# A new opening of a two-branch encoder layer: column groups for the gate rows, two key tiles in the modulation stages, and x scaled by token before it is transposed

## The reference

```python
mod = silu(c) @ w_ada + b_ada                      # six vectors of 1024: sh1, sc1, g1, sh2, sc2, g2
h = rmsnorm(x, norm_mix) * (1 + sc1) + sh1
proj = h @ w_in                                    # hq, hf, hi, hog, gq, gk, gv, ga, gb, gz, gate_a, gate_b
q, k, v = silu(causal_conv(gq, gk, gv))            # four taps; q and k are then l2-normed per head
log_a = -exp(a_log) * softplus(ga + dt_bias)       # ga, gb: 4 columns each, one per head
beta = sigmoid(gb)
y = sigmoid(gate_a) * (o_hg @ w_pa) + sigmoid(gate_b) * (o_gdn @ w_pb)
x = x + g1 * (y @ w_out)
x = x + g2 * swiglu(rmsnorm(x, norm_ffn) * (1 + sc2) + sh2)
```

## Time and profile before

| | |
|---|---|
| median of 3 runs | 943.8 us (943.55 to 945.01) |
| the profiled execution | 943.71 us, of which the span from first to last instruction is 941.9 us |
| PE busy | 919.7 us, 98% of the span |
| DVE, ACT, POOL busy | 71%, 47%, 11% |
| HBM read | 100 MB, 110 GB/s over the span |

### The profile page before, as it was taken

How to read it: one execution, slowest core, us unless ns; L and a number is a source line. 1 busy time by engine, 2 the same in 40 slices (tenths; PEclk the granted TensorE clock), 3 DMA queues, 4 the chain that set the end, 5 groups by cost and what they waited for, 6 DMA issues and landing times.

```text
span 941.9 us, 22445 instructions
## 1 busy us (share of the span) xinstructions
PE 919.7 (98%) x9425; PEld 892.4 (95%) x9425; DVE 670.0 (71%) x1254; ACT 446.8 (47%) x824; POOL 108.2 (11%) x135
## 2 busy tenths in 40 slices
PE   6999999999999999999999999999999999999997
PEld 6999888999999999999999999899999999999996
DVE  3778878866577677477766888899334899994454
ACT  6687445424234554753323267456212666663223
POOL 0110011112020110100100002122001222220000
PEclk9999999999999999999999999999999999999999
DMA  9824233344433422326643332232323343323312
GB/s 350 267 81 143 59 99 110 109 134 120 116 103 107 131 75 69 107 62 193 179 138 91 90 90 82 76 90 78 94 85 104 104 118 93 91 79 96 90 51 96
DMA packets 146031, 104.82 MB, mean 111 GB/s; under 512 B 5153, under 2 KB 138855, under 8 KB 144779
## 3 DMA queue, kind: packets, MB, share of 16 engines
q1 hardware_dynamic: 138955, 79.16, 28.8%
q0 software_dynamic: 6352, 22.00, 7.6%
q10 hardware_dynamic: 624, 2.23, 0.6%
HBM read 100.06 MB, written 3.31 MB: 110 GB/s over the span
## 4 chain that ended last, share of the span: by engine, by line
PE 84%; DVE 6%; ACT 4%; issue 3%; DMA 1%; SPq 1%; DVEq 0%; ACTq 0%
PE G L2210 58%; PE G L2305 15%; PE R L2218 10%; PE R L2221 1%; DMA wada<-in_w_ada_s 1%; DVE sum_lo L1755 1%; DVE w_sum L1746 1%; SPq L1097 1%; DVE cy L1881 1%; DVE cy L1878 1%; ACT w_hi L1347 0%; DVE cy L1882 0%; ACT d_hi L1352 0%; DVE w_lo L1755 0%; DVE cy L1877 0%
## 5 line engine op out<-in xcount | busy, mean ns | idle before, releaser
L2210 PE MATMUL G<-h_hi,w_hi 128*128 128x272 f32 (+1 forms) x880 | 263.6, 300 | 0.2 <-DVE ff_shift L2156 0.2
L2210 PE MATMUL G<-h_lo,w_hi 128*128 128x272 f32 (+1 forms) x880 | 253.7, 288 | 0.1
L2210 PE MATMUL G<-h_hi,w_lo 128*128 128x272 f32 (+1 forms) x880 | 253.6, 288 | 0.0
L1639 DVE TENSOR_TENSOR w_lo<-raw,w_hi 128x1024 fp32r<-128x1024 f32 (+3 forms) x111 | 118.8, 1070 | 82.0 <-ACT w_hi L1252 81.3
L2210 PEld LDWEIGHTS G<-h_hi,w_hi 128*128 128x128 f32 x880 | 165.7, 188 | 3.2 <-DVE ff_shift L2156 0.4
L2210 PEld LDWEIGHTS G<-h_lo,w_hi 128*128 128x128 f32 x880 | 166.0, 189 | 0.3 <-issue 0.3
L2210 PEld LDWEIGHTS G<-h_hi,w_lo 128*128 128x128 f32 x880 | 165.7, 188 | 0.0
L1252 ACT ACTIVATE w_hi<-raw 128x1024 fp32r<-128x1024 f32 (+3 forms) x111 | 101.5, 914 | 114.0 <-PE G L2210 113.9
L2305 PE MATMUL G<-x_hi,sum_hi 128*128 128x272 f32 x288 | 83.9, 291 | 1.9 <-ACT partial L1363 1.8
L2305 PE MATMUL G<-x_hi,sum_lo 128*128 128x272 f32 x288 | 83.4, 290 | 0.0
L2305 PE MATMUL G<-x_lo,sum_hi 128*128 128x272 f32 x288 | 82.9, 288 | 0.0
(11 more groups left out here) (335 smaller groups left out, 2117.4 us busy)
## 6 DMA issues: line engine op xcount, KB each, us to landing
raw<-in_w_in SPq DMA_DIRECT2D x48, 512.0 KB, 4.1
raw<-in_w_up SPq DMA_DIRECT2D x44, 512.0 KB, 4.0
w_ada<-in_w_ada_t POOLq DMA_DIRECT2D x49, 256.0 KB, 3.1
wada<-in_w_ada_s SPq DMA_DIRECT2D x8, 1024.0 KB, 14.2
raw<-in_w_down SPq DMA_DIRECT2D x14, 384.0 KB, 3.5
raw<-in_w_down SPq DMA_DIRECT2D x16, 320.0 KB, 3.1
raw<-in_w_out SPq DMA_DIRECT2D x8, 512.0 KB, 4.2
w_ada_t<-in_w_ada_t POOLq DMA_DIRECT2D x15, 256.0 KB, 3.1
```

The lines of the kernel that those rows point to most:

```text
L1639: dve.tensor_tensor(lo, raw[:, i % RAW, 0:job.nk, 0:job.m], hi.bitcast(F32), ALU.subtract).then_inc(w_lo_done, 1)
L2210: ins = pe.matmul(out, w, x, start=(job.first and k == 0 and p == 0), stop=(job.last and k == job.nk - 1 and p == 2))
```

## The change

Four edits. First, `x_sq` multiplies x itself by the roots on DVE, and `x_first` is a transpose on PE. Second, the gate columns ga and gb are no longer a job: their 8 columns are loaded once (`gab_w`), and a step `gab` multiplies them in float32 by `val`, a quarter of the tokens in each of four column groups of PE; `gab_sum` puts the quarters together with a selecting matrix, ACT copies the result to `acc`, and `gab_rows` does what DVE did in the evacuation of gagb. Third, the stages work on two key tiles, gk0 and gk1, and SP loads the second between the `w_ada` tiles of stages 1 and 2. Fourth, the order behind the opening is another. Job numbers are now gk0 0, gk1 1, gq0 2, gq1 3, and `taps` of gk0 and gk1 are placed by hand.

```diff
@@ make_plan, the opening
-    do("split", 0)
-    do("split", 1)
+    GK0, GK1, GQ0, GQ1 = range(4)
+    do("split", GK0)
     do("ada_rows", 0)
     do("ada_T", 0)
     do("h1", 0)
-    for j in range(1, STAGES):
-        do("ada_rows", j)
-        do("duo_part", 2 * j - 2, 0)
-        do("ada_T", j)
-        do("duo_part", 2 * j - 2, 1)
-        do("duo_part", 2 * j - 1, 0)
-        do("duo_part", 2 * j - 1, 1)
-        if j == STAGES - 1:
-            do("split_hi", 2)
-        do("h1", j)
-    do("split_lo", 2)
-    do("sel")
+    do("ada_rows", 1)
+    do("gab", 0)
+    do("part", GK0, (0,))
+    do("ada_T", 1)
+    do("part", GK0, (1,))
+    do("split", GK1)
+    do("h1", 1)
+    do("part", GK1, (0, 1))
+    do("gab", 1)
+    do("part", GK0, (2, 3))
+    do("ada_rows", 2)
+    do("part", GK1, (2,))
+    do("ada_T", 2)
+    do("part", GK1, (3,))
+    do("h1", 2)
+    do("ada_rows", 3)
+    do("gab", 2)
+    do("part", GK0, (4,))
+    do("ada_T", 3)
+    do("part", GK0, (5,))
+    do("part", GK1, (4, 5))
+    do("h1", 3)
+    do("gab", 3)
+    do("part", GK0, (6, 7))
+    do("split_hi", GQ0)
+    do("part", GK1, (6, 7))
@@ make_plan, behind the opening
-    duo(gagb, gk0)
-    around(gk1, [("g_sp",), ("split_hi", 4), ("g_a",), ("split_lo", 4)], [])
-    around(gq0, [("g_sq", 0, 2), ("g_scan",)], [])
-    around(gq1, [("g_sq", 0, 3), ("g_norm", 0, 2)], [("g_rows",), ("c_load",)])
+    mark = len(plan)
+    gk0()
+    gk1()
+    del plan[mark:]
+    do("evac", 0)
+    do("split_lo", GQ0)
+    do("gab_sum")
+    around(gq0, [("split_hi", GQ1), ("taps", 0, 0), ("taps", 0, 1), ("gab_rows",), ("split_lo", GQ1), ("evac", 1),
+                 ("sel",), ("g_sp",), ("taps", 1, 0), ("taps", 1, 1), ("g_a",)], [])
+    around(gq1, [("g_scan",), ("g_sq", 0, 2), ("g_sq", 0, 3), ("g_norm", 0, 2)], [("g_rows",), ("c_load",)])
...
-        if x[0] == "conv":
+        if x[0] == "conv" and g > 1:
@@ SP
+            sp.dma_start(gab_w[:, :, 0:2 * NH], t["w_in"][:, COL["gagb"]:COL["gagb"] + 2 * NH]
+                         .rearrange("(k p) m -> p k m", p=P)).then_inc(gab_in, 16)
             load(0)
-            load(1)
             for j in range(STAGES):
+                if j == 2:
+                    load(1)
                 for v in range(2):
                     sp.dma_start(wada01[:, j, v, :, :], t["w_ada_s"][j, v]).then_inc(ada_in[j], 16)
+            sp.dma_start(gab_sel[:, :, :], t["gate_select"]).then_inc(const_in, 16)
@@ DVE
-                    dve.tensor_scalar(x_diag[0:L, c, 0:L], ident[0:L, 0:L], rn_tok[0:L, CHUNKS + c:CHUNKS + c + 1], None,
-                                      ALU.mult).then_inc(diag_ready, 1)
+                    dve.tensor_scalar(xtok[0:L, c, :], xtok[0:L, c, :], rn_tok[0:L, CHUNKS + c:CHUNKS + c + 1], None,
+                                      ALU.mult).then_inc(x_scaled_in, 1)
...
                 elif name == "h1":
                     dve.wait_ge(gain_ready, a[0] + 1)
+                    if a[0]:
+                        dve.wait_ge(gab_done, a[0])
@@ PE
+                elif name == "gab":
+                    j, b = a[0], first_fill[spot("gab", STAGES - 1)] % 4
...
+                    for k in (2 * j, 2 * j + 1):
+                        pe.wait_ge(val_ready, k + 1)
+                        for q in range(4):
+                            ins = pe.matmul(R[q * QUAD:(q + 1) * QUAD, b, 0:QUARTER], gab_w[:, k, :],
+                                            val[:, k % 2, q * QUARTER:(q + 1) * QUARTER], start=k == 0, stop=k == KD - 1,
+                                            skip_group_check=True)
+                    ins.then_inc(fill_done if j == STAGES - 1 else gab_done, 1)
+                elif name == "gab_sum":
...
+                    for h in range(2):
+                        fill(n, h, [mm(lambda b, q=q: R[0:QUAD + NH, b, q % 2 * QUARTER:(q % 2 + 1) * QUARTER], gab_sel[:, q, :],
+                                       gab_parts) for q in (2 * h, 2 * h + 1)])
...
-                        fill(n, f, [mm(lambda b, j=j: R[:, b, j * L:(j + 1) * L], xtok[0:L, c, k * P:(k + 1) * P],
-                                       x_diag[0:L, c, 0:L]) for j, k in enumerate(ks)])
+                        fill(n, f, [tr(lambda b, j=j: R[:, b, j * L:(j + 1) * L], xtok[0:L, c, k * P:(k + 1) * P])
+                                    for j, k in enumerate(ks)])
```

More of the change, by code:

```diff
@@ L39 @@
 HALF = TOK // 2
+QUARTER = TOK // 4
 NH = 4
@@ L563, in bank_users @@
         "vectors": ["dve"] * 2, "x_first": ["act", "dve"] if name == "x_first" and a[0] < N_CHUNK else ["act"], "sums": ["act"] * 2, "onorm": ["act"] * 2,
-        "ada_rows": ["act"], "ada_T": ["dve"], "g_rows": ["dve"], "g_norm": ["act"] * 2, "g_bcast": ["act"] * n, "g_gram": ["dve"] * n,
+        "ada_rows": ["act"], "ada_T": ["dve", None, None] if name == "ada_T" and a[0] < STAGES - 1 else ["dve"],
+        "gab": ["act"] if name == "gab" and a[0] == STAGES - 1 else [], "gab_sum": ["act"] * 2, "g_rows": ["dve"], "g_norm": ["act"] * 2, "g_bcast": ["act"] * n, "g_gram": ["dve"] * n,
         "g_tok": ["act"] * n + ["dve"] * n, "g_row": ["dve"] * n,
@@ L589, in build @@
         for user in bank_users(step):
+            if user is None:
+                freed.append(("dve", count["dve"]))
+                continue
             count[user] += 1
@@ L1102, in _ @@
             for n, step in enumerate(plan):
-                if step[0] == "job" or step[0] == "duo" and step[1]:
+                if step[0] == "job" or step[0] == "duo":
                     for i in step[1:]:
@@ L1171, in _ @@
                     pool.memset(T64[0:P // 2, :, :], 0.0).then_inc(inverse_zero, 1)
-                    wait_group(pool, groups_at["gagb", 0])
+                    pool.wait_ge(fill_done, last_bank[spot("gab_sum")] + 1)
                     pool.memset(Um[:, :, :, :], 0.0).then_inc(inverse_zero, 1)
@@ L1240, in split_weights @@
                 wait_weights(act, i)
[L1241 to L1247, removed]
                 if i in aside:
@@ L1414, in _ @@
                     read_banks(n, 0, [(ada_rows[:, a[0] % 2, :], lambda b: R[:, b, 0:P])])
+                elif name == "gab" and a[0] == STAGES - 1:
+                    read_banks(n, 0, [(gab_parts, lambda b: R[:, b, 0:QUARTER])])
+                elif name == "gab_sum":
+                    read_banks(n, 0, [(x, lambda b: R[0:QUAD + NH, b, 0:HALF]) for x in q_halves(acc[0:QUAD + NH, :])])
                 elif name == "ogate":
@@ L1429, in _ @@
                     ln_exp_tables()
-                    wait_slot(act, groups_at["gagb", 0])
+                    wait_bank(act, last_bank[spot("gab_sum")])
                     act.activation(rows[:, 2, :], acc[QUAD:QUAD + NH, :], ACT.Exp, scale=-1.0)
@@ L1533, in _ @@
                     kind, arg, _ = groups[g]
[L1534 to L1538, removed]
+                    if kind == "conv":
                         what, pair, h, slot = arg
@@ L2180, in _, with fill @@
             seen = dict(s=0, lo=0)
-            def fill(n, k, products):
+            def fill(n, k, products, banks=1):
                 f = first_fill[n] + k
@@ L2309, in _ @@
                     ins.then_inc(q_done, 1)
-                elif name == "duo_part":
-                    both = duos[0]
-                    if a[0] == 0:
-                        pe.wait_ge(w_lo_done, nth_split[both[a[1]]] + 1)
-                    products(*[(both[a[1]], half) for half in range(2)], ks=(a[0],))
+                elif name == "part":
+                    i, ks = a
+                    if ks[0] == 0:
+                        pe.wait_ge(w_lo_done, nth_split[i] + 1)
+                    products((i, 0), (i, 1), ks=ks)
+                elif name == "gab":
+                    j, b = a[0], first_fill[spot("gab", STAGES - 1)] % 4
+                    if j == 0:
+                        pe.wait_ge(gab_in, 16)
+                        pe.wait_ge(pad_zero, 1)
+                        wait_bank(pe, last_bank[spot("x_first", N_CHUNK - 1)])
+                        assert last_bank[spot("x_first", N_CHUNK - 1)] % 4 == b
+                    for k in (2 * j, 2 * j + 1):
[5 more added lines that the diff above has]
+                    ins.then_inc(fill_done if j == STAGES - 1 else gab_done, 1)
+                elif name == "gab_sum":
+                    pe.wait_ge(ones_set, 1)
+                    pe.wait_ge(const_in, 48)
+                    wait_bank(pe, last_bank[spot("gab", STAGES - 1)])
+                    for h in range(2):
+                        fill(n, h, [mm(lambda b, q=q: R[0:QUAD + NH, b, q % 2 * QUARTER:(q % 2 + 1) * QUARTER], gab_sel[:, q, :],
+                                       gab_parts) for q in (2 * h, 2 * h + 1)])
                 elif name == "first_chunks":
@@ L2320, in _ @@
                 elif name == "duo":
-                    if a == duos[0]:
-                        pe.wait_ge(ones_set, 1)
-                        pe.wait_ge(const_in, 32)
```

(7 more changed lines are left out.)

66 lines of the change are left out of this document (29 added, 37 removed).

## The result

The changed kernel takes 959.0 us (median of 4 runs, 957.7 to 960.8), the kernel before 944.4 beside it, so the medians are 14.6 us apart (959.2 were predicted). The ratio of the two kernels is 1.0142, 95% interval 1.0117 to 1.0167; that stands for 13.4 us (11.0 to 15.8), so the two measures agree only to about 1 us. The profiled execution took 959.75 us, its span is 957.9, 16.0 longer than before.

A forecast was written before the change was run, and what follows sets the result against it. PE's queue was taken to bound the kernel, with the ACT and DVE string nearly equal from 48 to 95 us. 943.7 + 11.9 (wait) + 2.6 (restart) + 1.0 (slow opening) = 959.2 us, range 951 to 964.

The forecast's parts named there:

- Part 1, x: Ahead of stage 1: transposes replacing 40 float32 products save nothing, covered by the load; bounds 0 to 1 us later.
- Part 2, PE's work: Opening: gagb job of 6.0 us removed, gate products of 0.5 per stage and gab_sum of 1.1 added; 2.8 us saved.
- part 3: End of the opening: gk0 ends at 45.2, gab_sum at 47.7; PE gains about 0.9 us, the rest becomes waits.
- Part 5: Clock: PE's slow restart after the 13 us wait costs 2.6 us; a slow stage 1 adds 1.0.
- Part 4, the order and the wait: Between gq1's halves: a 25.2 us ACT and DVE string delays gk0's square to 70.4; PE waits 13 us, net 11.9.
- The restart, 2.6: After PE's wait in gq1: PE starts slowly, priced at 2.6 us, bounds 0 and 2.6.
- The first rival: Whole kernel: no clock loss anywhere, 955.6 us; chance 0.2.
- The second: Rival on the opening: first stages run slow throughout, opening ends 2.6 rather than 1.0 us late, 960.8 us; chance 0.15.
- The third: Rival on gq1: square ready by about 57 us, no wait, 942.8 to 940.9; chance 0.05 faster, 0.03 no change.
- The fourth: Rival on the gate products: column groups don't overlap, 2.0 us instead of 0.5 per stage, 963.7 us; chance 0.04.

The follow-up runs named there:

- the filled run with gk1 behind: Mended-order kernel with gk1's chunks after gk0's last one instead of in the stages, plus 14 filling products in stage 3: 946.1 us, ratio 1.0004.
- The run with the order mended: Changed kernel with gk0's square and the scan moved from inside gq1 to ahead of gq0's taps: 949.5 us, ratio 1.0048.
- the filled wait: Changed kernel with 100 more products on PE ahead of the first g_norm's wait: 956.1 us, ratio 1.0122.
- with x by the diagonal: Changed kernel with the x edit alone undone, so PE multiplies x by small diagonals again: 963.0 us, ratio 1.0194.
- both kernels with the filling: 14 unneeded products in stage 3, added to the kernel with one key tile in the stages (947.6 us, 1.0020) and that with gk1 behind gk0 (946.1 us, 1.0004).
- the run with the 86: The filled run with gk1 behind, plus 86 transposes of 32x32 at PE's idle start: 946.5 us, ratio 1.0011.
- one key tile: Changed kernel with gk1 taken out of the stages as an ordinary job and the old order behind them: 949.9 us, ratio 1.0041.
- second tile behind: Mended-order kernel with gk1's chunks behind gk0's last one instead of between the stages, without filling: 948.1 us, ratio 1.0027.
- With 40 more ahead, both kernels: Changed kernel with the x edit undone (963.0 us, ratio 1.0194), and changed kernel with 40 small transposes at PE's start (964.1 us, ratio 1.0184).

## Why the prediction was right

**Part 1, x, at nothing.** Shown: alone in the kernel before it gives 0.9998 (0.9985 to 1.0010). A scaling took 0.75 us where 0.92 was taken.

**Part 2, PE's work.** `gab_sum` took 1.12 us (1.1 predicted), four gate products 0.44, so nearly 0.9 per stage where 0.5 was taken: 0.11 us a product, not the 0.06 of the modulation rows. That the saving would mostly go into waits was right, with one change: part 3 sent it to `val` and the split of gk1 (2.3 + 0.9 us of waits, as shown), and the filled run with gk1 behind shows that without these it goes into waits for the loads.

**Parts 3 and 5, the opening.** ACT's `w_hi`, which waits for gk0's last product, starts at 46.41, so gk0 ended about 46.2, 1.0 after the 45.2 of part 3. Part 5 had added 1.0, for a slow clock at stage 1. The size was right by luck and the reason wrong here: stage 1's rows take 1.99 us, full pace. (They were slow, 3.36 to 3.52 us, in three kernels with small transposes added at the start, behind waits of 2.18 to 3.13 us for the load.) The step that failed is the end of stage 3 in part 3: from the transpose at 40.30 to the gate products that wait for the second `val`, 44.16, it is 3.86 us where 3.4 was taken, and the transpose came 0.25 late. That and the longer gate products make most of the 1.0. gq0 began at 48.87 where 47.7 was forecast, so the 0.9 us that PE was to gain in the opening didn't come.

**Part 4, the order and the wait.** From gk0's end (ACT starts at 46.41) to `g_norm` at 71.47 it is 25.1 us; 25.2 predicted, and the wait is 13.3 of 13. That the sum came out to 0.1 us is luck in part: DVE's gate rows took 1.6 us instead of 2.5, and ACT's branch of gk1's evacuation, `sel` and `g_sp`, said to end "just before" DVE's, ended after it, as DVE's 0.81 us wait for ACT at 58.08 shows. The run with the order mended shows that it is the order: 8.9 of 13.4 us go with two steps moved. It also shows what stands right behind: with the wait gone, gv0's low part waits next, 1.3 us.

**The restart, 2.6.** 2.57 by the filled wait. The first rival (955.6, no clock loss) falls with it and with the clock of 0.50. The second (slow stages) falls as stage 1's rows run at full pace. Stage 0's did take 3.64 us, but in this order it costs nothing: with x by the diagonal they took 1.96, stage 1 then waited 1.89 us for its load, and the last gate products came at the same time (44.15). By the rule of the Trainium skill ("TensorE: Matmul & The Clock Gate", Part 4) that transposes don't count for the clock, stage 0's rows should be slow behind them in every run. They took 3.64 us in the changed kernel, and 1.95 with the same transposes in both kernels with the filling and no transposes at the start, so the runs don't bear it out. In the run with the 86 the last 16 transposes of x took 1.68 us and the first 16 took 3.67, with nothing but transposes on PE up to there. The third (not slower) needed the square at 57; even in the mended order `g_norm` waited for it until 59.07. The fourth falls: the column groups overlap, 0.11 us a product against 0.28 in `gab_sum`, which has no column groups, though not so well as was taken.

**What the sum left out** is small: 0.7 to 0.8 us in each of two stops in mid-fill (below) against one of 0.46 before, given back in part by steps behind the square that wait no more.

## What to carry to other kernels

When PE runs ahead of ACT and DVE, what it is spared is idle time: look first at what ends last in that stretch, here the loads and then one string over ACT and DVE, and spare that. When work is moved into a tighter place, write the in-order queue of each engine out again: a step that is ready but stands behind others (the square behind taps and scan) costs as much as one that is late. And read where in the trace two kernels part before believing that an edit caused a difference of 0.5%.

## What was not expected of the hardware

PE stopped in mid-fill with no semaphore, in the changed kernel too, where 68 records of 32x32 follow one another:

```profile
128.46 0.51 PE L2234 MATMUL R<-Xc,Uc 32*32 32x32 f32 x32 [0.69 <-issue]
...
133.06 0.72 PE L2234 MATMUL R<-Xc,Uc 32*32 32x32 f32 x56 [0.83 <-issue]
```

With the same 9409 records in the program, stops stand with 32 and 56 records of a fill left in four kernels (the changed one, order mended, one key tile, second tile behind), 0.53 to 0.72 and 0.26 to 1.35 us long. With 40 more ahead, both kernels have one of 1.7 us, followed by half clock; the first one's ratio is 0.0052 over that of the changed kernel, 4.9 us. What PE waits for there is not shown; that it is its instructions is a guess.

Half clock came after short waits too: 0.86 and 1.12 us with four gate products between them (1.97 us for `gab_sum` instead of 1.12), 1.74 us for an evacuation, or 1.7 us among small products. It didn't come after every such wait (1.54 us for the same evacuation, clock 1.00; up to 2.03 us ahead of the stages, rows in 1.95). What a wait costs can then be more than its length.
